# Mixing stage: six squares moved to step 0, one product to step 2, and a gate product in three parts

## What is computed

```python
def finish(hh, s):                       # mLSTM
    o = jax.nn.sigmoid(s["ml_o"].astype(F32)).reshape(hh.shape)
    y = head_layernorm(o * hh, norm_g.reshape(ML_HEADS, ML_DH))
    return y.reshape(*y.shape[:2], -1) * jax.nn.silu(s["ml_z"])
...
def finish(y, xh, s):                    # SSD
    y = y + d_skip[:, None] * xh
    y = y.reshape(bs, t, SSM_D_INNER) * jax.nn.silu(s["ss_z"])
    y = rmsnorm(y.reshape(bs, t, SSM_GROUPS, SSM_D_INNER // SSM_GROUPS), norm_g.reshape(SSM_GROUPS, -1))
...
def finish(o, s):                        # HGRN2
    o = rmsnorm(o, norm_g.reshape(HG_HEADS, HG_DV))
    return o.reshape(*o.shape[:2], -1) * jax.nn.silu(s["hg_z"])
```

## Time and profile before

| | us |
|---|---|
| median of 3 runs | 5609.52 |
| lowest and highest run | 5601.59, 5609.97 |
| profiled execution, its own time | 5606.4 |
| its span, first to last instruction | 5604.5 |
| mixing, first layer: first to last L2123 (18 tiles) | 1298.15 to 1828.72 |
| mixing, second layer: first to last L2123 (16 tiles) | 4100.19 to 4565.95 |

### The profile page before, as it was taken

How to read it: one execution, slowest core, us unless ns; L and a number is a source line. 1 busy time by engine, 2 the same in 40 slices (tenths; PEclk the granted TensorE clock), 3 DMA queues, 4 the chain that set the end, 5 groups by cost and what they waited for, 6 DMA issues and landing times. The chain is left out here.

```text
span 5604.5 us, 66026 instructions
## 1 busy us (share of the span) xinstructions
PE 5110.7 (91%) x23797; PEld 2574.2 (46%) x23912; DVE 2836.9 (51%) x4708; ACT 1865.4 (33%) x4089; POOL 2467.9 (44%) x1686
## 2 busy tenths in 40 slices
PE   6999999877888899998989999998588879999989
PEld 2454544455665433332444545444556643333334
DVE  2443435336777555551335346363467765555324
ACT  1222222214444244444012223222244433444422
POOL 0212232314444299998111322323244436899931
PEclk8999999968889799999999999999588888999999
DMA  5443533483221100000433444344632220000032
GB/s 189 134 146 139 169 125 131 151 248 121 99 84 64 54 1 9 8 7 32 178 126 123 148 142 145 136 134 134 197 124 98 84 77 1 8 1 8 5 120 105
DMA packets 415701, 561.23 MB, mean 100 GB/s; under 512 B 103160, under 2 KB 288048, under 8 KB 411024
## 3 DMA queue, kind: packets, MB, share of 16 engines
q1 hardware_dynamic: 395650, 516.59, 27.7%
q10 hardware_dynamic: 19728, 40.41, 1.9%
HBM read 402.54 MB, written 154.06 MB: 99 GB/s over the span
## 5 line engine op out<-in xcount | busy, mean ns | idle before, releaser
L2520 POOL TENSOR_TENSOR attention_PS<-attention_PS 128x1024 f32<-128x1024 f32 x548 | 1265.6, 2354 | 81.4 <-ACT attention_PS L2653 73.6
L2566 DVE TENSOR_REDUCE attention_mxp<-psum 128x1 f32<-128x512 f32 (+1 forms) x1016 | 654.3, 686 | 541.2 <-PE psum L2703 541.2
L2653 ACT ACTIVATE attention_PS<-psum 128x512 f32<-128x512 f32 (+1 forms) x1168 | 630.7, 591 | 717.1 <-PE psum L2757 694.6
L2703 PE MATMUL psum<-attention_QK 32*128 32x512 f32 (+1 forms) x2592 | 771.6, 611 | 9.1 <-DVE attention_mxp L2555 6.1
L657 POOL TENSOR_TENSOR projection_cx<-projection_cx,projection_cw 128x1152 f32<-128x1152 f32 x72 | 194.9, 2707 | 1178.7 <-DMA projection_cx<-xbc 532.6
L2751 PE MATMUL psum<-attention_QK 32*128 32x512 f32 x2336 | 664.6, 642 | 0.0
L2769 PE MATMUL psum<-attention_PS,attention_va 128*64 128x512 f32 x2336 | 627.7, 616 | 0.0
L680 PE MATMUL psum<-group_B,projection_hT 128*128 128x512 f32 (+1 forms) x1360 | 571.2, 564 | 37.0 <-ACT projection_p L819 20.8
L680 PE MATMUL psum<-group_B,projection_S 128*128 128x512 f32 (+1 forms) x1360 | 556.3, 552 | 2.3 <-DVE projection_u L994 2.3
L680 PE MATMUL psum<-projection_T,projection_S 128*128 128x512 f32 (+1 forms) x1360 | 556.4, 552 | 0.0
L680 PEld LDWEIGHTS psum<-group_B,projection_hT 128*128 128x128 f32 x1360 | 263.1, 195 | 305.7 <-issue 264.6
(11 more groups left out here) (397 smaller groups left out, 7484.0 us busy)
## 6 DMA issues: line engine op xcount, KB each, us to landing
group_B<-in_w_in SPq DMA_DIRECT2D x120, 512.0 KB, 7.1
group_B<-in_w_in SPq DMA_DIRECT2D x48, 1024.0 KB, 8.9
projection_cx<-xbc SPq DMA_DIRECT2D x216, 192.0 KB, 3.3
u<-projection_u SPq DMA_DIRECT2D x158, 256.0 KB
mixing_hg<-u SPq DMA_DIRECT2D x34, 1024.0 KB, 5.0
u<-projection_u SPq DMA_DIRECT2D x52, 512.0 KB
output_y<-y SPq DMA_DIRECT2D x34, 512.0 KB, 3.2
xc<-projection_cx SPq DMA_DIRECT2D x72, 192.0 KB, 1.9
```

Of the source, the lines that this page charges most:

```text
L2520: G.tensor_tensor(SA[x % 2][:, rs, 0:w], one[:, rs, 0:w], PT[i % PTB][:, rs, 0:w], ALU.add) \
L2566: bk.release(V.tensor_reduce(mxp[x % 2][:, q:q + nn, 2 * pr + j, a], bk[job, j][:, 0:nn * (hi - lo)].rearrange("p (q n) -> p q n", q=nn), ...
L2653: bk.release(A(PT[i % PTB][:, r, 0:w], bk["st", i, r][:, 0:w], ACT.Exp, scale=scale), ("st", i, r))
L2703: return T(out[:, at:at + hi - lo], QK[rows(r), a0, t * P:(t + 1) * P], QK[rows(r), 2 + a0, lo:hi], start=True, stop=True)
```

## The change

Four edits, all inside `mixing`. In ScalarE's stream the mLSTM and SSD squares of tile t-1 leave `statistics` (step 2) and form `first_squares`, called in step 0 behind the drain of bcT; the HGRN2 squares stay in step 2. VectorE's kh moves from step 1 to step 2, between lg and sP. GpSimd's product yo is cut into three of 256 columns, in steps 4, 5 and 6; what waits for it counts three per tile, and VectorE waits for its part before it writes that part of Y again. GpSimd's preparation of zg moves from step 5 to step 7, and ScalarE's stores of yo from step 5 to step 7.

```diff
-                def finish(t):
+                def finish(t, n):
...
-                    G.tensor_tensor(yo[t % 2][:], Y[:], zg[:], ALU.mult).then_inc(s["y_ready"], 1)
+                    G.tensor_tensor(yo[t % 2][:, n], Y[:, n], zg[:, n], ALU.mult).then_inc(s["y_ready"], 1)
...
-                        if v == 4 and t:
-                            finish(t - 1)
-                        if v == 5:
+                        if v in (4, 5, 6) and t:
+                            finish(t - 1, v - 4)
+                        if v == 7:
                             if t:
-                                gp.wait_ge(s["y_ready"], t)
+                                gp.wait_ge(s["y_ready"], 3 * t)
                             G.tensor_copy(zg[:, 1], gn[:, 1])
                             G.tensor_tensor(zg[:, 0], og[b][:, 1], gn[:, 0], ALU.mult)
...
-                def statistics(t):
+                def first_squares(t):
                     act.wait_ge(s["hm_ready"], t + 1)
                     act.wait_ge(s["yss_ready"], t + 1)
+                    for h in range(H):
+                        st.mark(A(sq[:, 0, h * 64:h * 64 + 64], Y[:, 0, h * 64:h * 64 + 64], ACT.Square, accum_out=ssq[:, h:h + 1]))
+                    for g in range(2):
+                        st.mark(A(sq[:, 1, g * P:g * P + P], Y[:, 1, g * P:g * P + P], ACT.Square, accum_out=ssq[:, 4 + g:5 + g]))
+
+                def statistics(t):
                     bk.freed(act, ("out", t))
                     for h in range(H):
-                        A(sq[:, 2, h * 64:h * 64 + 64], Y[:, 2, h * 64:h * 64 + 64], ACT.Square, accum_out=ssq[:, 8 + h:9 + h])
-                    for g in range(2):
-                        st.mark(A(sq[:, 1, g * P:g * P + P], Y[:, 1, g * P:g * P + P], ACT.Square, accum_out=ssq[:, 4 + g:5 + g]))
-                    for h in range(H):
-                        st.mark(A(sq[:, 0, h * 64:h * 64 + 64], Y[:, 0, h * 64:h * 64 + 64], ACT.Square, accum_out=ssq[:, h:h + 1]))
+                        st.mark(A(sq[:, 2, h * 64:h * 64 + 64], Y[:, 2, h * 64:h * 64 + 64], ACT.Square, accum_out=ssq[:, 8 + h:9 + h]))
...
                             drain(("bcT", t), f2(bcT[:]))
+                            if t:
+                                first_squares(t - 1)
...
-                        if v == 5 and t:
+                        if v == 7 and t:
                             store(t - 1)
+                first_squares(count - 1)
                 statistics(count - 1)
...
-                        if v == 1:
-                            bk.freed(dve, ("sum", t))
-                            V.tensor_tensor(kh[:], hcol(t, "hg_k"), eh[:], ALU.mult).then_inc(s["kh_ready"], 1)
                         if v == 2:
                             if t + 1 < count:
                                 lowest(t + 1)
+                            bk.freed(dve, ("sum", t))
+                            V.tensor_tensor(kh[:], hcol(t, "hg_k"), eh[:], ALU.mult).then_inc(s["kh_ready"], 1)
                             bk.wait(dve, ("S", t))
```

More of the change, by code:

```diff
@@ L1858, in _ @@
                             gp.sem_inc(s["pool_done"], 1)
-                finish(count - 1)
+                for n in range(3):
+                    finish(count - 1, n)
             @block.scalar
@@ L1927, in store @@
                 def store(t):
-                    act.wait_ge(s["y_ready"], t + 1)
+                    act.wait_ge(s["y_ready"], 3 * t + 3)
                     act.dma_start(k.y[t + skipped, :, 0:256], yo[t % 2][:, 0]).then_inc(s[f"y_stored{t % 2}"], 16)
@@ L2022, in outputs @@
                     bk.wait(dve, ("out", t))
+                    if t:
+                        dve.wait_ge(s["y_ready"], 3 * t)
                     ins = V.tensor_copy(Y[:, 2].rearrange("p (a x w) -> p x a w", a=2, x=2),
@@ L2121, in _ @@
                             if t:
-                                dve.wait_ge(s["y_ready"], t)
+                                dve.wait_ge(s["y_ready"], 3 * t - 2)
                             st.then(V.tensor_tensor(hm.rearrange("p (a x w) -> p x a w", a=2, x=2),
@@ L2140, in _ @@
                             bk.wait(dve, ("ssown", t))
+                            if t:
+                                dve.wait_ge(s["y_ready"], 3 * t - 1)
                             ins = V.tensor_tensor(yss, bk["ssown", t][:, 0:256], dx[:], ALU.add)
```

## The result

The change makes the kernel faster, by less than forecast: median 5565.94 us of four runs (5556.26 to 5577.75) against 5605.56 of four of the kernel before (5595.82 to 5609.97). The ratio is 0.9933, 95% interval 0.9906 to 0.9959, so 39.6 us are gained where about 80 were forecast. The profiled execution took 5577.75 us, the highest of the four; against 5606.4 before it gains 28.7. Mixing gains 19.7 and 11.9 in its two stretches, and the rest of the program is some 3 us longer.

The account below looks back on a forecast made before the run. A loop of waits through ScalarE's late squares, plus TensorE's lowered clock, bounds mixing. A tile becomes 29.40 - 1.54 + 0.1 + 0.6 = 28.56 us; 81.8 us less gives 5524.6, or 5528 in the runs' terms; range 5495 to 5585.

Parts of the forecast that it names:

- the loop: Loop of waits that sets a mixing tile's length, about 29.4 us at full clock; forecast 28.56 us after the change.
- The wait for rstd: Sign: VectorE's wait for ScalarE's rstd falls from 2.2 us a tile to about 0.7 or less.
- that before `own`: Sign: TensorE's wait before `own` in step 4, for VectorE's num, falls from 0.79 to 0.2 to 0.4 us.
- that before the increments: Sign: TensorE's 0.92 us wait for ScalarE's L drain, before L2293, is gone.
- The squares: Six squares leave step 2 for ScalarE's idle time, taking 1.54 us off a tile; bounds 0.92 and 1.71.
- The meetings on VectorE: Step 7: zg's GpSimd products run beside VectorE's L2145 and L2146, costing 0.6 us a tile; bounds 0 and 1.44.
- kh: VectorE's kh lands ahead of sP in step 2, costing 0.1 us a tile; bounds 0 and 0.43.
- the clock: TensorE's clock stays up once step 4's idle spells shrink from 1.71 to 0.2 us; remaining price 0, otherwise 1.7 a tile.
- the clock falls as before: Rival, chance 0.20: TensorE's clock still falls, so only the loop counts, 43 us gained, 5567.
- the slower rival: Rival, chance 0.08: clock falls at TensorE's wait for Aw ahead of step 0, 3.8 us a tile, 5649.
- no meeting: Rival, chance 0.10: GpSimd's products don't meet VectorE's instructions; 27.96 us a tile, 102 us gained, 5509.

Follow-up runs that it names:

- squares and kh: The change with only its squares and kh edits: product whole in step 4, zg and stores in step 5 as before; 5509.46 us, ratio 0.9837 to the kernel before.
- the last experiment: Squares and kh moved, product and zg as before, step 6's three exponent matmuls done twice; 5523.24 us, ratio 0.9865 to the kernel before.
- doubled set in step 7: The change with the three exponent matmuls of step 7 done twice, ahead of the wait for Aw; 5533.45 us, ratio 0.9878 to the kernel before.

## Why the prediction was wrong

*The direction and the loop were right.* The wait for rstd is 0.43 in the short tile (7.6 / 17 on the mean; forecast 0.7 or less), that before `own` is 0.22, that before the increments is gone. The timeline of that short tile, in steps 3 and 4:

```profile
1348.43 0.96 DVE L2038 TENSOR_TENSOR mixing_Y<-mixing_Y,mixing_rstd 128x768 f32<-128x768 f32 x1 [0.43 <-ACT mixing_rstd L1928]
...
1350.12 0.34 PE L2302 MATMUL psum<-mixing_va,mixing_kp 128*64 128x65 f32 x4
...
1351.07 2.00 PE L2313 MATMUL psum<-mixing_va,mixing_sP 128*128 128x65 f32 x16 [0.22 <-DVE mixing_num L2087]
```

`own` takes 2.00 us at full clock behind these short spells. The squares fitted into ScalarE's idle time: alone they bring the short tile from 29.40 to 27.86 us, just the 1.54 that were priced.

*The meetings on VectorE* were priced at 0.6 us with bounds 0 and 1.44. Measured: 0.86 + 0.83 - 0.85 = 0.84 on VectorE, and between the short tiles of the change and of squares and kh 28.60 - 27.87 = 0.73. The Trainium skill (SBUF — State Buffer, Who interferes with whom) was quoted for an exclusion over a whole instruction, by which 1.44 would have been due. That both VectorE instructions stretch while GpSimd's products run agrees with its rule; but each is longer by 0.43 and 0.41 us only, less than one product of 0.72, so the price was under the bound.

*kh* was priced at 0.1 and is worth nothing that can be measured (27.87 us a short tile with it moved, 27.86 without).

*The step that failed is the clock*: its term was put at nothing, with "no other place in the short tile holds such a pair, so I take 0". The clock of the stretches rose from 0.89 and 0.90 to 0.94 and 0.93 only. The pair in step 4 indeed sets off nothing in the change, the last tiles aside. But the short tile holds a wait of 1.54 us in step 6, and the short tile of before had one too:

```profile
1394.89 0.71 PE L2324 MATMUL psum<-mixing_xw,mixing_xc 128*128 128x128 f32 x4 [1.75 <-DVE mixing_ysum L2133]
```

In the change the clock fell behind that wait in 8 of 32 tile periods. The size: the seven mid-layer tiles with a fall are some 5.2 us above a short one, so 7 x 5.2 = 36 us; the last periods of both layers, 37.63 and 32.66 us, the eighth fall in the first of them, add 9.0 + 4.1 = 13. Together that is 49 of the 53 us missing between the forecast 81.8 and the 28.7 of the profiled execution. The falls are long with the meetings; with zg in step 2 they last 3.4 us. That the spread of the change's runs, 21 us, is some four falls more or fewer (21 / 5.2) is not shown, since one run's trace was kept; the mean granted clock agrees, with 0.936 and 0.935 in the two longer runs and 0.941 in the two shorter.

*The rivals.* The measured 5566 is almost the 5567 of "the clock falls as before", by another way, so this is luck: step 4 is free of falls. What came is the mechanism of the slower rival in fewer tiles (8 of 32, not two in three), at 5.2 us each rather than 3.8, and its trigger was put one step late: the wait for Aw, named there, does not set it off (no fall at 1.4 us in the last experiment) but goes with its length. "In the short tile the waits of step 6 to 0 are there and the clock is 1.00" was no evidence against it: the short tile was chosen for its clock. And "no meeting", 5509, is what the change gives when the GpSimd edits are left out, 5509.46; that it agrees so closely is luck too, for seven short falls are in it.

*Open:* why the fall comes in some tiles and not in others with the same wait, and what exactly ends it. With kh back in step 1, tiles of the same length and waits had five falls in the first layer and one in the second. In three runs the falls come evenly, some 58, 113 and 140 us apart (doubled set in step 7; squares and kh; zg in step 2), which is every second, fourth and fifth tile, so it is hardly chance; in the change they don't. Nor was the wait in step 6 parted from the short matmuls right ahead of it, which every kernel here has. The runs show the place and that less idle time behind it goes with shorter falls, in two ways (zg away, or useless matmuls), no more.

## What to carry to other kernels

When a wait that pulls the clock down is taken out, go through every other wait of that engine in the loop, and the ones that the edit lengthens, before the clock's price is put at nothing; a tile that kept its clock proves little. A move of GpSimd work into "idle" time has to be laid over VectorE's order there: here two meetings of 0.4 us cost some 60 us (5565.94 against 5504.80 with zg in step 2). About 26 of them are the loop, 32 x (28.60 - 27.78) between the short tiles; the rest went with the clock, as the wait that they made stood behind the spot where it fell. Try one edit of a bundle at a time: here one of four carries the gain, and another takes back more than half of it.

## What was not expected of the hardware

Matmuls that compute nothing new made kernels faster: the one before by 32 us (5569.28 against 5601.26), the change by some 70 (5494.77 against 5565.94, in part because they also parted zg from VectorE). In another kernel they made new meetings and cost 14 us (5523.24 against 5509.46). And a fall of TensorE's clock has no fixed length here: 3.4 us where at most 0.28 us of waiting for Aw followed in the same tile, about 14 where 0.69 to 1.11 us did.
